# Other places for block 1's half points in the mixer blocks of a streaming attention and retention kernel

## The chip, the cores and the metric

The kernel is one program on one core of a Trainium2 chip. The metric is the device time of one execution in microseconds (us), and the median over the runs is what is compared. The engines are named as in the profile: PE (TensorE), DVE (VectorE), ACT (ScalarE), POOL (GpSimd, which here only issues gathers) and SP (which only issues other transfers).

## The reference, cut to what matters

One inference step of an encoder layer over nine blocks of 128 tokens: block 0 holds the sample rows, blocks 1 to 8 the prompt. All arrays are float32.

```python
h  = rmsnorm(x);  z = h @ w_in                       # q, k, v of A; q, k, v, gate of B; branch gates
oa = sliding_window_attention(z, sinks)              # mixer A, 8 heads, ALiBi, softmax
ob = groupnorm(retention(z)) * silu(z_rg)            # mixer B, 4 heads, state carried from block to block
x  = x + (sigmoid(ga) * (oa @ w_branch_a) + sigmoid(gb) * (ob @ w_branch_b)) @ w_out
h2 = rmsnorm(x)
idx, gate = top16_of_product_keys(h2 @ w_q)          # 8 heads x 16 experts = 128 rows a token
act = gelu(h2 . peer_u[idx])                         # "dots"
y  = x + sum_k gate_k * act_k * peer_v[idx_k]        # "values"
```

A mixer block takes the z of 128 tokens through attention, retention, the merge of the two branches and the output projection. The experts of a token block need 128 gathered rows of `peer_u` and 128 of `peer_v` for each token.

## The kernel before, in words

The kernel runs in stages. The one in question is the mixers of blocks 2 to 8. It is written as one Python loop per engine, so the order on each engine is fixed by hand, and semaphores tie the engines together. In the same stage runs what is left of block 1's expert work: 80 gathered rows of `peer_u` and 80 of `peer_v` for each token. It is cut into groups of three rows and spread over the mixer blocks as "half points".

`dve_point(v, blk, j)` (j from 0 to 7) is one half point. An odd j takes the dots of one group: three multiply-and-sum instructions (line 1472) over the buffers `ru`. An even j takes the values of a group that is four groups older: three multiply-and-add instructions (line 1489) over the buffers `rv`, and point 0 also one small product (line 1480). There are three buffers for each kind. So POOL may issue the three gathers of the next group only after the three instructions of this one are done. POOL's order is fixed, too: for each group number first the values' gathers (line 1508), then the dots' gathers (line 1516). Block 2 has only the dots; the last group of dots, in block 8, has two rows.

The order on DVE in `dve_block` for block b, with what the other engines do:

- copies of the transposed q and k (from line 689), which need PE's transposes (line 308) of this block; then block b-1's gating (line 429) and biases (line 433)
- point 0; then the scores are scaled and masked (lines 711 and 712, they need PE's line 623), `atm` is formed (line 714), row maxima (line 389 and on)
- ACT's exponentials (line 353) run, DVE takes point 1 and then waits for them (line 399); ACT scales the probabilities
- points 2 and 3; then `dve_merge` of block b-1 (lines 438 to 441), which needs PE's two branch products (lines 324 and 327). PE starts those when `atm` is written
- points 4 and 5; then the retention norm (lines 410 to 422), which needs PE's line 647
- points 6 and 7; then `dve_residual` of block b-1 (line 446), which needs PE's output product (line 340); the state update (line 735), which needs line 653; the second norm (lines 450 to 454)

PE's order in a block is: transposes (308), gated transposes of b-1 (315), scores (623, 346), branches of b-1 (324, 327), transposes of the probabilities (632), transposes of the merge (333), attention output (640), retention (646, 647), output product of b-1 (340), state product (653), then a wait for the retention norm.

SP's queue copies 40 parts of the expert table (`uv_d`, 1 MB each, lines 244 and 245), eight parts in each of the blocks 3 to 7, two at a time: after the load of the next keys part; after the probabilities (`prob`); after the merge's transposes (`mixt`), behind the next gates; and after the retention (`ro`).

```python
                        if blk > 2:
                            rest_of_table(sp, part, part + 2)
                            sp.wait_ge(s["prob"], blk + 1)
                            rest_of_table(sp, part + 2, part + 4)
```

After block 8 the stage closes with the last groups of values, block 1's output, the key search of block 2's tokens and the last merge; then the expert stage of blocks 2 to 8 begins.

## Time and profile before

| what | value |
|---|---|
| median of 3 runs | 4177.75 us (4168.81 to 4183.3) |
| the profiled execution | 4131.7 us, span 4129.9 us |
| granted TensorE clock, mean | 0.928 |
| busy share of the span | PE 80%, DVE 59%, POOL 43%, ACT 26% |
| bytes moved | 1563 MB, mean 378 GB/s |
| mixer stage of blocks 2 to 8 | from about 1165 to about 1676 us |

Times in the rows are us from the start of the span. A row of the timeline gives start, duration, engine, line, operation, output and inputs, and the count of instructions that it merges. In brackets stands how long the engine sat idle before it and on what. A releaser that begins with DMA is a transfer that landed late. Names of buffers carry the stage's suffix; `CUSTOM_DVE_ANT_0` is the dot instruction.

### The profile page before, as it was taken

To read this page: it belongs to the slowest core of one execution; us is meant where nothing else is said; L and a number is where in the kernel's file an instruction comes from. 1 tells how busy PE (TensorE), PEld (TensorE's weight loads), DVE (VectorE), ACT (ScalarE), POOL (GpSimd) and SP (SyncE) were. 2 spreads that over 40 slices of the span, in tenths; PEclk is the share of its full clock that TensorE was granted. 3 is DMA by queue.
4 is the path that set the end of the run, shared out by engine and by line. 5 is a ranking of instruction groups with operands and counts; after the bars stand their busy time and mean duration, and the time that the engine had idled before them with its cause. 6 is when DMAs were issued, how large, how long until landed. Compare 5 with 4: busy or idle time off the path is not lost.

```text
span 4129.9 us, 32128 instructions
## 1 busy us (share of the span) xinstructions
PE 3298.1 (80%) x8957; PEld 1643.4 (40%) x8957; DVE 2455.5 (59%) x4977; ACT 1088.2 (26%) x2932; POOL 1769.1 (43%) x1588
## 2 busy tenths in 40 slices
PE   8775589999928878749779779878878977977776
PEld 5453256666524444324224323323323423422222
DVE  0122168998857677544864764674684585485454
ACT  2102011111113233213333333333333333323322
POOL 1020137787723333114444454444444444445554
PEclk9876799999958888969999999999999999999999
DMA  9898899999999998469999999999999999999998
GB/s 352 297 290 310 321 304 413 411 407 414 412 360 341 344 354 300 160 269 420 421 421 418 415 420 399 421 414 409 420 409 409 419 417 403 422 406 422 422 422 353
DMA packets 303586, 1563.05 MB, mean 378 GB/s; under 512 B 31280, under 2 KB 59184, under 8 KB 179888
## 3 DMA queue, kind: packets, MB, share of 16 engines
q0 software_dynamic: 228096, 1300.34, 78.7%
q1 hardware_dynamic: 60736, 239.86, 15.0%
q10 hardware_dynamic: 14592, 21.10, 1.4%
q8 instruction: 51, 0.84, 0.1%
q14 instruction: 111, 0.91, 0.1%
HBM read 1517.54 MB, written 179.04 MB: 411 GB/s over the span
## 4 chain that ended last, share of the span: by engine, by line
DMA 26%; PE 18%; issue 7%; DVE 4%; ACT 1%; POOL 1%; POOLq 0%; ACTq 0%; DVEq 0%
DMA ring<-uv_d,IXD_p 26%; PE ps L1807 14%; PE ps L1779 3%; DVE ring L1906 2%; ACT dg L1850 1%; DVE BV_p L979 1%; POOL ring L2012 1%; ACT GE_p L1844 0%; DVE BP_p L984 0%; DVE CA_p L989 0%; DVE VV_p L1332 0%; DVE CA_p L1397 0%; DVE DOT_p L1906 0%; DVE ACC L1887 0%; PE ps L1796 0%
## 5 line engine op out<-in xcount | busy, mean ns | idle before, releaser
L1807 PE MATMUL ps<-ring,dg 128*128 128x512 f32 x3584 | 1704.6, 614 | 474.3 <-ACT dg L1850 449.9
L2012 POOL DMA_INDIRECT ring<-uv_d,IXD_p x896 | 1082.3, 1208 | 1318.1 <-PE ps L1807 1068.0
L1906 DVE CUSTOM_DVE_ANT_0 ring<-ring,H 128x1024 f32<-128x1024 f32 x896 | 1094.2, 1223 | 907.3 <-DMA ring<-uv_d,IXD_p 886.6
L1807 PEld LDWEIGHTS ps<-ring,dg 128*128 128x128 f32 x3584 | 664.0, 194 | 1432.8 <-ACT dg L1850 714.3
L1238 PE MATMUL ps<-w,xg 128*128 128x368 f32 x1792 | 554.3, 472 | 2.0 <-ACT SC_s L936 2.0
L1844 ACT ACTIVATE GE_p<-DOT_p 128x2 f32<-128x2 f32 x448 | 91.1, 203 | 1502.6 <-DVE DOT_p L1906 1502.6
L1238 PEld LDWEIGHTS ps<-w,xg 128*128 128x128 f32 x1792 | 340.4, 190 | 215.5 <-ACT SC_s L936 2.2
L1850 ACT ACTIVATE dg<-gdi,GE_p 128x128 f32<-128x128 f32 x896 | 310.6, 393 | 46.6 <-ACT GE_p L1844 1.2
L1838 ACT ACTIVATE gdi<-ident,GD_p 128x128 f32<-128x128 f32 x896 | 303.1, 386 | 26.3 <-issue 19.9
L145 POOL DMA_DIRECT2D uv_d<-in_peer_u x88 | 45.6, 518 | 504.7 <-DMA uv_d<-in_peer_v 270.3
L1779 PE MATMUL ps<-wq,hT_p 128*128 128x512 f32 x384 | 197.9, 597 | 0.0
L1508 POOL DMA_INDIRECT rv<-in_peer_v,IXD x80 | 88.4, 1105 | 231.6 <-DVE AC L1489 215.2
L969 POOL DMA_INDIRECT ring_s<-in_peer_v,IXD_s x128 | 158.2, 1236 | 44.9 <-issue 38.4
L1101 DVE CUSTOM_DVE_ANT_0 ring_s<-ring_s,H_s 128x1024 f32<-128x1024 f32 x128 | 152.1, 1223 | 41.6 <-DMA ring_s<-in_peer_u,IXD_s 40.5
L969 POOL DMA_INDIRECT ring_s<-in_peer_u,IXD_s x128 | 152.6, 1192 | 47.3 <-issue 40.2
L226 PE MATMUL ps<-w,xg 128*128 128x368 f32 x512 | 161.4, 479 | 13.9 <-DMA w<-in_w_in 13.9
L1112 DVE SCALAR_TENSOR_TENSOR ACC_s<-ring_s,WG_s,ACC_s 128x1024 f32<-128x1024 f32 x126 | 157.1, 1290 | 13.3 <-DMA ring_s<-in_peer_v,IXD_s 12.9
L1267 ACT ACTIVATE zo<-ps,rstd 128x368 f32<-128x368 f32 x112 | 61.8, 566 | 373.4 <-PE ps L1238 371.9
L1516 POOL DMA_INDIRECT ru<-in_peer_u,IXD x80 | 82.1, 1027 | 151.7 <-DVE DOT L1472 117.1
L1472 DVE CUSTOM_DVE_ANT_0 ru<-ru,H 128x1024 f32<-128x1024 f32 x80 | 96.0, 1222 | 60.0 <-DMA ru<-in_peer_u,IXD 59.9
L226 PEld LDWEIGHTS ps<-w,xg 128*128 128x128 f32 x512 | 98.6, 193 | 76.0 <-issue 16.3
L1489 DVE SCALAR_TENSOR_TENSOR AC<-rv,WG,AC 128x1024 f32<-128x1024 f32 x80 | 102.7, 1284 | 40.8 <-DMA rv<-in_peer_v,IXD 36.1
(415 smaller groups left out, 2901.7 us busy)
## 6 DMA issues: line engine op xcount, KB each, us to landing
uv_d<-in_peer_u POOLq DMA_DIRECT2D x88, 512.0 KB, 5.4
uv_d<-in_peer_v POOLq DMA_DIRECT2D x88, 512.0 KB, 6.6
w<-in_w_in SPq DMA_DIRECT2D x8, 2944.0 KB, 15.1
w<-in_w_in SPq DMA_DIRECT2D x16, 1472.0 KB, 9.8
z_d<-zo ACTq DMA_DIRECT2D x16, 1288.0 KB, 18.8
uv_d<-in_peer_u SPq DMA_DIRECT2D x40, 512.0 KB, 9.6
uv_d<-in_peer_v SPq DMA_DIRECT2D x40, 512.0 KB, 11.3
ring<-uv_d,IXD_p POOLq DMA_INDIRECT x896, 11.2
```

The lines of the kernel that those rows point to most:

```text
L226: mm = T.matmul(ps[:, m % AB, 0:WC], xg0[:, k, b * P:(b + 1) * P], w0[:, p % 2, n % 2, k, :], start=(k == 0), stop=(k == KT - 1))
L969: gather = g.indirect_dma_start(ring[:, n % RING, :], None, t["peer_u"] if kind == "u" else t["peer_v"], bass.IndirectOffsetOnAxis(ap=inde ...
L1101: V.tensor_tensor_reduce(out=row, in0=row, in1=H2[:], scale=1.0, scalar=0.0, op0=ALU.mult, op1=ALU.add, accum_out=DOT[:, k:k + 1]).then_in ...
L1112: V.scalar_tensor_tensor(ACC[:, k % 2], row, WG[:, k:k + 1], ACC[:, k % 2], ALU.mult, ALU.add).then_inc(d["freed"], 1)
L1238: mm = T.matmul(ps[:, n % AB, 0:WC], xg[:, k, b * P:(b + 1) * P], w[:, tile % 2, k, :], start=(k == 0), stop=(k == KT - 1))
L1489: V.scalar_tensor_tensor(AC1[:], row, WG1[:, k:k + 1], AC1[:], ALU.mult, ALU.add).then_inc(d["accz"], 1)
L1779: mm = T.matmul(bank(2 + n), hT[:, k, :], wq[:, k, n * 512:(n + 1) * 512], start=(k == 0), stop=(k == KT - 1))
L1807: mm = T.matmul(bank(6 + n), dg[:, k % DR, :], ring[:, k % RS, D + n * 512:D + (n + 1) * 512], start=(k == 0), stop=(k == NK - 1))
L1838: S.activation(gdi[:, k % GR, :], ident[:], ACT.Copy, scale=GD[:, k:k + 1]).then_inc(e["gdi"], 1)
L1850: S.activation(dg[:, k % DR, :], gdi[:, k % GR, :], ACT.Copy, scale=GE[:, k:k + 1]).then_inc(e["diag"], 1)
L1906: V.tensor_tensor_reduce(out=row, in0=row, in1=H2[:], scale=1.0, scalar=0.0, op0=ALU.mult, op1=ALU.add, accum_out=DOT[:, k:k + 1]).then_in ...
L2012: g.indirect_dma_start(ring[:, n % RS, :], None, uv_d, bass.IndirectOffsetOnAxis(ap=IXD[:, n:n + 1], axis=0)).then_inc(s_ring[n % RS], 16)
```

## The change

The half points keep their order among themselves and their content, and no instruction is added or removed. Their places in DVE's order are changed in each of the blocks 2 to 8. Point 1 goes ahead of the scores, point 2 into the wait for the exponentials, points 4 and 5 ahead of the merge, points 6 and 7 ahead of the retention norm.

```diff
-            dve_point(v, blk, 0)
+            for half_point in range(2):
+                dve_point(v, blk, half_point)
             if blk <= 2:
                 v.wait_ge(s_mask, 16 * 4 + 48 * blk)
             v.wait_ge(s["scores"], blk + 1)
...
             dve_softmax(v, blk, 2 * P, sink[:], step)
-            dve_point(v, blk, 1)
+            dve_point(v, blk, 2)
             dve_probs(v, blk, 2 * P, False)
-            for half_point in range(2, 4):
+            for half_point in range(3, 6):
                 dve_point(v, blk, half_point)
             if merge:
                 dve_merge(v, blk - 1)
-            for half_point in range(4, 6):
+            for half_point in range(6, 8):
                 dve_point(v, blk, half_point)
             v.wait_ge(s["oat"], blk + 1)
             V.tensor_copy(kaT[:, 0], kaT[:, 1])
             V.tensor_copy(va[:, 0], va[:, 1])
             dve_retention_norm(v, blk, 2, step)
-            for half_point in range(6, 8):
-                dve_point(v, blk, half_point)
             if merge:
                 dve_residual(v, blk - 1)
```

## Rows read from the trace of the kernel before

**Rows 1.** DVE's timeline in block 4, from its first copy to block 5's:

```profile
1309.77 0.68 DVE L689 COPY qbT_p<-ps 128x512 f32<-128x512 f32 x1
...
1316.79 4.06 DVE L1489 SCALAR_TENSOR_TENSOR AC<-rv,WG,AC 128x1024 f32<-128x1024 f32 x3
1321.20 1.22 DVE L711 SCALAR_TENSOR_TENSOR Pr_p<-ps,alibi_p 128x1024 f32<-128x1024 f32 x1 [0.35 <-PE ps L623]
...
1326.73 1.22 DVE L1472 CUSTOM_DVE_ANT_0 ru<-ru,H 128x1024 f32<-128x1024 f32 x1
...
1331.03 0.23 DVE L399 TENSOR_TENSOR rs_p<-rs_p,es_p 128x8 f32<-128x8 f32 x1 [0.78 <-ACT Pr_p L353]
...
1348.19 1.22 DVE L438 TENSOR_TENSOR gates_p<-gates_p,ps 128x1024 f32<-128x1024 f32 x1 [7.82 <-PE ps L327]
...
1379.56 1.23 DVE L1472 CUSTOM_DVE_ANT_0 ru<-ru,H 128x1024 f32<-128x1024 f32 x1 [0.80 <-DMA ru<-in_peer_u,IXD]
...
1380.71 1.22 DVE L446 TENSOR_TENSOR X_p<-X_p,ps 128x1024 f32<-128x1024 f32 x1
...
1384.98 0.68 DVE L689 COPY qbT_p<-ps 128x512 f32<-128x512 f32 x1
```

**Rows 2.** PE's timeline in block 4:

```profile
1324.21 10.14 PE L324 MATMUL ps<-wa_p,oaT_p 128*128 128x512 f32 x16 [1.04 <-DVE atm_p L714]
...
1351.85 1.09 PE L333 MATMUL ps<-ident,gates_p 128*128 128x128 f32 x8 [2.03 <-DVE gates_p L441]
1352.88 3.33 PE L640 MATMUL ps<-Pr_p,va 128*64 128x128 f32 x32
...
1373.42 1.89 PE L653 MATMUL ps<-zv_p,kdec_p 128*128 128x256 f32 x8
```

**Rows 3.** DVE's timeline, first copy and merge of block 3; end of block 7:

```profile
1236.81 0.68 DVE L689 COPY qbT_p<-ps 128x512 f32<-128x512 f32 x1
...
1273.62 1.22 DVE L438 TENSOR_TENSOR gates_p<-gates_p,ps 128x1024 f32<-128x1024 f32 x1 [4.70 <-PE ps L327]
...
1602.37 1.22 DVE L446 TENSOR_TENSOR X_p<-X_p,ps 128x1024 f32<-128x1024 f32 x1
...
1606.64 0.68 DVE L689 COPY qbT_p<-ps 128x512 f32<-128x512 f32 x1
```

**Rows 4.** PE's timeline, the state product of block 7:

```profile
1597.88 1.89 PE L653 MATMUL ps<-zv_p,kdec_p 128*128 128x256 f32 x8
```

**Rows 5.** Timeline of SP and POOL in block 4, first table copy, last gather:

```profile
1334.86 0.49 SPq L244 DMA_DIRECT2D uv_d<-in_peer_u  x1
...
1339.09 0.94 POOL L1508 DMA_INDIRECT rv<-in_peer_v,IXD  x1 [0.30 <-issue]
```

**Rows 6.** The tile rv, the gather issued at 1339.09 alone:

```profile
DMA to landing us min/median/max: 10.7/10.7/10.7
```

**Rows 7.** DVE's timeline at the end of block 8:

```profile
1670.55 1.22 DVE L446 TENSOR_TENSOR X_p<-X_p,ps 128x1024 f32<-128x1024 f32 x1 [5.33 <-PE ps L340]
```

**Rows 8.** Timeline of PE and POOL at the end of block 2:

```profile
1227.44 0.94 POOL L1508 DMA_INDIRECT rv<-in_peer_v,IXD  x1 [0.30 <-issue]
...
1231.82 3.01 PE L308 MATMUL ps<-ident,zqk_p 128*128 128x128 f32 x13 [18.59 <-DMA zqk_p<-z_d]
```

**Rows 9.** Block 2: busy of PE, PEld, DVE, ACT, POOL; PE clock, DMA share, GB/s:

```profile
1167.00:1232.00 65.00, 25.86 (x110) 22.32 (x111) 23.70 (x52) 15.12 (x34) 13.37 (x15) 0.58 1.00 400
```

**Rows 10.** DMA queues from 1165 to 1232: packets, MB, share:

```profile
q0 software_dynamic: 1713, 6.28, 23.4%
```

**Rows 11.** PE's timeline, in block 2 and behind block 8:

```profile
1201.85 6.00 PE L640 MATMUL ps<-Pr_p,va 128*64 128x128 f32 x32 [2.03 <-ACT Pr_p L676]
...
1715.28 3.68 PE L1546 MATMUL ps<-ident,zv_p 128*128 128x128 f32 x16 [5.33 <-ACT zv_p L1572]
```

**Rows 12.** PE in two stretches: length, PE busy, granted clock, DMA share, GB/s:

```profile
1575.20:1580.00 4.80, 4.80 (x34) 0.64 0.80 272
...
1715.30:1719.00 3.70, 3.70 (x17) 0.50 0.00 0
```

## The prediction

> **What bounds the kernel now.** The page of the profile says that the last stage, the experts of blocks 2 to 8, is nearly all transfers. The change does not touch that stage, so it moves the end only by moving its start. I therefore read the timeline of the mixer stage, engine by engine, and laid the landing of each gather beside it. Times below that begin with a plus are us behind the first copy (line 689) of a block.
>
> From block 3 to block 8 there are five turns, 369.8 us together [rows 3]. In block 4 the order of waits is this [rows 1, 2]. At +11.4 DVE has finished point 0 and waits 0.35 for the scores. At +17.0 it begins point 1, and still waits 0.78 for the exponentials. At +38.4, 7.8 late, it gets PE's branch products for the merge. At the end it waits for rows: the last dot of point 7 starts at +69.8, the moment its row has landed, and the residual follows at +70.9. The residual's own partner, PE's output product, ended where the state product begins, at +63.65. So the residual is 7.3 late for points 6 and 7. Over the five turns these lags are 6.6, 7.3, 6.8, 5.9 and 4.5, 31.1 in all (block 4's pair in [rows 1, 2], the last in [rows 3, 4]). Block 8 is different: there the residual waits 5.3 for PE, and PE bounds it [rows 7].
>
> **The change, part by part.** Nothing is added or removed: 80 dots of 1.22 and 80 values of some 1.3 us stay, and with them the gathers that POOL issues behind their semaphores. What changes is what stands ahead of what.
>
> *Points 6 and 7 ahead of the retention norm.* The norm's result is wanted by PE only after the state product, so there are some 10 us of cover. The residual can then start 0.2 behind PE's output product, as in block 8, instead of 31.1 late over five turns: 30.1 less. But the state update waits for the state product, which takes 1.9 [rows 2], where it now follows the residual at once, after 1.2. That gives 0.6 back in each block, as read from block 8's residual and update. Gain: 27.1 in five turns, 0 in block 8.
>
> *Point 1 ahead of the scores.* Three dots at a pitch of 1.15 are 3.4; DVE had 0.35 to spare there. So scores, `atm` and all behind them come 3.0 later: PE's branches start on `atm`, SP's second table copies start on the scaled probabilities. All of PE's chain to the output product hangs on that: 3.0 in each of six blocks, 15.0 in the five turns and 3.0 in block 8.
>
> *Point 2 in the exponentials' wait.* Three values take 4.0 until the next instruction may start. Point 1 and the wait had filled 4.3 there [rows 1]. Its gathers go out at +11.9 and have landed at +18.4 to +22.4 in all blocks, while point 2 wants them from +20.0 on, one each 1.3. No cost. If they were as late as the gathers that fly beside a table copy (10.7, [rows 6]), it would be 3.
>
> *Points 4 and 5 ahead of the merge.* The time to beat is PE's: +38.4 in block 4, +36.8 in block 3 [rows 1, 3], 37.6 on the mean of the five, plus the 3.0. DVE has time for the instructions; what counts is when rows land. Point 3 ends at +28.3, so POOL issues point 5's gathers at +29.1 to +31.6. SP's table copies now start at +28.15 (+25.1 before, and 3.0). In the kernel before, point 4's gathers have just this place: they follow 1.55 behind the first table copy of 1334.86, and the last goes out at 1339.09 and lands 10.7 later, 14.9 behind that copy [rows 5, 6]. In five blocks this distance is 14.3 to 14.9. What is in flight beside them is the same in both kernels: the end of one group, two parts of the table, this group. So point 5's last row lands at +42.75, the dot takes 1.22, and the merge starts at +44.0. That is 44.0 - 40.6 = 3.4 late on the mean: 17.1 in five turns. In block 8 point 5 has two rows, and other loads stand in place of the copies; the second row would land at +41.7 and the merge start at +42.9 instead of +41.4: 1.5. The bounds: 0 if the rows land as early as a gather does at the median (8.1 us), 3.4 + 1 if the half microsecond of queueing that I can't see adds up.
>
> *PE's clock.* PE waits for the merge 2.0 us now, at the full clock of 2.4 GHz [rows 2]. After the change it waits 4.6 to 6.3 in blocks 3 to 7 and 3.5 in block 8. After a wait of 5.33 the trace shows the granted clock at 0.50, that is 1.2 GHz, and 16 transposes took 3.68 [rows 11, 12]. Costs of such a fall: in block 7 it came at a wait of 2.0 already (granted 0.64 in that stretch) and cost some 1.6, block 6 likewise. If lines 333 and 640 run wholly at half clock, 640 takes 6.00 for 3.33 [rows 2, 11] and 333 about 0.9 more: 3.6. From below it is 0. I take 2.0, near to what was measured, in blocks 3 to 5, and 0.5 more in blocks 6 and 7, which have paid already: 7. At the start of a block PE's clock is low anyway, and is again.
>
> *Block 2.* It has dots only, and all of its transfers are squeezed: the share is 1.00 at 400 GB/s [rows 9]. Its points waited for rows one after another. Point 1 now fits whole into DVE's wait for block 2's scores, so each later group is asked for some ten us earlier. DVE doesn't gain by it. Block 3 starts when the keys part has landed, at 1231.8 [rows 8], and that load shares the engines with the gathers. Before, four groups had come through by then (6.28 MB, 1.57 each, [rows 10]) and the first values were only issued at 1227.4 [rows 8]. Now those values and the first dots of block 3 are also in flight ahead of it: up to 3.1 MB, 7.7 us at 400 GB/s. From below: if the keys part isn't delayed, block 3 starts 1.9 earlier, since DVE is no longer in the way. I take 5 later. The Trainium skill ("DMA: Bandwidth & Descriptors", on queues, rings and completion order) has each engine take turns between the queues that have work, a packet at a time. By that rule the gathers get half the engines while they last, the keys part is pushed back by nearly all of their bytes, and the term would be 6 to 7. By the lower bound of the rows it would be -1.9.
>
> **Sum.** -27.1 + 15.0 + 17.1 = +5.0 for the five turns; +4.5 for block 8; +7 for the clock; +5 for block 2: +21.5, all ahead of the expert stage, with nothing to absorb it. The profiled execution took 4131.7, 46 less than the median; I carry the difference over to the median: 4177.75 + 21.5 = 4199.
>
> **The rivals.** *A, the rows are in time (not slower).* If point 5's last row lands by +39.4, the merge doesn't wait for DVE, PE's clock stays, and what was gained at the block's end is kept: -27.1 + 15.0 + 2 + 3.0 - 1.9 = -9, 4169. For it speaks the median latency of 8.1. Against it is that in five blocks out of five the gathers behind this table copy took 14.3 to 14.9 behind its start. It decides at a merge start of about +42 on the mean: below, the five turns gain.
>
> *B, the clock holds.* The merge is late, but PE keeps 2.4 GHz over the wait: 7 less, +14.5, or +7.6 if block 2 gives nothing either: 4185 to 4192. For it speaks that block 4 passed its wait of 2.0 at full clock [rows 2]; against it the wait of 5.33 [rows 11].
>
> *C, the clock falls at every merge and stays low.* 3.6 in each block and, if it lasts to the retention or the output product, the 3.2 that line 324 pays for its slow start (10.14 for 16, against 6.9 at the pitch of the fast ones [rows 2]): up to 6.8 in place of 2, so 30 to 45 in all, 4208 to 4223. The Trainium skill ("TensorE: Matmul & The Clock Gate", on oscillation) says that a wait between two bursts, repeated in each turn of a loop, makes PE go cold in every one of them. By that rule all six blocks pay; the trace agrees for the wait of 5.33 and shows two of six already at 2.0.
>
> **Chances.** The forecast 0.46, with its own range +12 to +30; A 0.17; B 0.23; C 0.14. 0.3% is 12.5 us, about what runs of this kernel can tell. Slower by more than that: the forecast but for 0.03 of it, C, and 0.10 of B: 0.67. Within: 0.29. Faster: 0.04, the part of A that ends beyond its -9. The range goes from 4176, most of A left out, to 4222, C's end.
>
> **What would show it.** In the changed kernel, per block from 3 on: no idle time ahead of line 446 but for PE's line 340, and the residual right behind that product; line 711 three us later, with no wait for line 623; no wait for ACT at line 399; a wait for a `ru` row just ahead of the merge, the merge at +43 to +45, and no wait for line 327; PE's wait ahead of line 333 at 4.6 to 6.3; block 3's first copy near 1242; turns of 74 to 78 where they were 73 to 75. The forecast is wrong if the merge starts before +42, if PE's line 333 and 640 stay at 1.09 and 3.33 everywhere, or if block 3 begins by 1236.

## The result, and the profile after

| kernel | median of 8 runs | range |
|---|---|---|
| before | 4172.27 us | 4166.05 to 4183.59 |
| after | 4207.49 us | 4197.64 to 4232.85 |

The changed kernel takes 1.0092 times as long (95% interval 1.0064 to 1.012): 35 us slower by the two medians. Predicted were +21.5 and 4199 us, with a range up to 4222. Two executions in the chip's slower state, 4603 us of p67_only and 4193 us of late7_head, are in no ratio and no median below. In the changed kernel the lines behind 711 are one or more off (711 is 712, 1472 is 1471, 1489 is 1488, 1508 is 1507); lines 308 to 699 are the same.

DVE's timeline in block 4 of the changed kernel, to compare with [rows 1]:

```profile
1379.53 0.68 DVE L689 COPY qbT_p<-ps 128x512 f32<-128x512 f32 x1
...
1393.97 1.22 DVE L712 SCALAR_TENSOR_TENSOR Pr_p<-ps,alibi_p 128x1024 f32<-128x1024 f32 x1
...
1403.79 0.17 DVE L399 TENSOR_TENSOR rs_p<-rs_p,es_p 128x8 f32<-128x8 f32 x1 [0.23 <-ACT Pr_p L353]
...
1409.78 1.28 DVE L1488 SCALAR_TENSOR_TENSOR AC<-rv,WG,AC 128x1024 f32<-128x1024 f32 x1 [2.03 <-DMA rv<-in_peer_v,IXD]
1415.29 1.29 DVE L1488 SCALAR_TENSOR_TENSOR AC<-rv,WG,AC 128x1024 f32<-128x1024 f32 x1 [4.22 <-DMA rv<-in_peer_v,IXD]
1418.33 1.28 DVE L1488 SCALAR_TENSOR_TENSOR AC<-rv,WG,AC 128x1024 f32<-128x1024 f32 x1 [1.75 <-DMA rv<-in_peer_v,IXD]
1420.84 1.23 DVE L1471 CUSTOM_DVE_ANT_0 ru<-ru,H 128x1024 f32<-128x1024 f32 x1 [1.23 <-DMA ru<-in_peer_u,IXD]
...
1423.43 1.23 DVE L1471 CUSTOM_DVE_ANT_0 ru<-ru,H 128x1024 f32<-128x1024 f32 x1 [1.36 <-DMA ru<-in_peer_u,IXD]
...
1425.81 1.22 DVE L438 TENSOR_TENSOR gates_p<-gates_p,ps 128x1024 f32<-128x1024 f32 x1
...
1453.66 1.22 DVE L446 TENSOR_TENSOR X_p<-X_p,ps 128x1024 f32<-128x1024 f32 x1 [9.30 <-PE ps L340]
...
1458.53 0.68 DVE L689 COPY qbT_p<-ps 128x512 f32<-128x512 f32 x1
```

The end of the turn is what was forecast: the residual (line 446) waits for PE's product alone, and no row is late there. The price stands ahead of the merge. The scores come at +14.4 instead of +11.4, without a wait; then five rows in a row are late, and the merge starts at +46.3, where PE's branches end at +40.0. DVE stood idle for 10.6 us in front of it, all for rows. The last row of point 5 is not one of them: it was there when DVE came to it, at +45.1.

PE's timeline in the same block, to compare with [rows 2]:

```profile
1396.97 8.86 PE L324 MATMUL ps<-wa_p,oaT_p 128*128 128x512 f32 x16 [4.04 <-DVE atm_p L715]
...
1429.47 1.97 PE L333 MATMUL ps<-ident,gates_p 128*128 128x128 f32 x8 [8.16 <-DVE gates_p L441]
1431.37 4.87 PE L640 MATMUL ps<-Pr_p,va 128*64 128x128 f32 x32
...
1453.46 1.89 PE L653 MATMUL ps<-zv_p,kdec_p 128*128 128x256 f32 x8
```

And two stretches of it: length, busy time of PE, PEld, DVE, ACT and POOL, then the granted clock, DMA share and GB/s:

```profile
1421.50:1429.40 7.90, 0.00 (x0) 0.00 (x0) 6.51 (x10) 1.79 (x2) 4.24 (x5) 0.68 0.79 245
1429.50:1436.10 6.60, 6.60 (x40) 6.16 (x40) 6.39 (x8) 1.02 (x1) 2.33 (x3) 0.61 0.97 308
```

PE does nothing for 7.9 us, and the granted clock falls meanwhile. Line 333 then takes 1.97 where it took 1.09, line 640 4.87 for 3.33. Read in finer stretches, the granted clock is 1.00 from 1421.6 to 1423, 0.50 from 1425 to 1434 and 1.00 again from 1436.2.

The timeline of SP and POOL in block 4, to compare with [rows 5]:

```profile
1407.56 0.49 SPq L244 DMA_DIRECT2D uv_d<-in_peer_u  x1
...
1404.37 1.89 POOL L1507 DMA_INDIRECT rv<-in_peer_v,IXD  x1 [4.55 <-DVE AC L1488]
1406.57 1.99 POOL L1507 DMA_INDIRECT rv<-in_peer_v,IXD  x1 [0.30 <-issue]
1408.86 0.94 POOL L1507 DMA_INDIRECT rv<-in_peer_v,IXD  x1 [0.30 <-issue]
1410.11 1.77 POOL L1515 DMA_INDIRECT ru<-in_peer_u,IXD  x1 [0.30 <-issue]
1412.18 0.94 POOL L1515 DMA_INDIRECT ru<-in_peer_u,IXD  x1 [0.30 <-issue]
1413.43 0.94 POOL L1515 DMA_INDIRECT ru<-in_peer_u,IXD  x1 [0.30 <-issue]
```

The copies go out at +28.0, as predicted. POOL issues point 4's values and point 5's rows, six gathers, as one train around them. Three of the six take 1.8 to 2.0 us to issue instead of 0.94, so the last goes out at +33.9.

The load of the next keys part in block 2, in the kernel before and in the changed one, and the start of block 3 in the changed one, to compare with [rows 8]:

```profile
1212.55 2.30 SPq L751 DMA_DIRECT2D zqk_p<-z_d  x1
...
1275.28 1.19 SPq L750 DMA_DIRECT2D zqk_p<-z_d  x1
...
1298.63 3.00 PE L308 MATMUL ps<-ident,zqk_p 128*128 128x128 f32 x13 [24.44 <-DMA zqk_p<-z_d]
...
1301.67 0.69 DVE L689 COPY qbT_p<-ps 128x512 f32<-128x512 f32 x1 [3.96 <-PE ps L308]
```

Block 2 started at 1234.81 here. The keys part lets PE begin 63.8 behind that, where it was 56.7 before. Of these 7.1, 3.0 are that SP asks for the part later, at +40.5 instead of +37.5, and 4.1 that PE gets it 23.4 behind that instead of 19.3. DVE's first copy then follows sooner, so block 2's turn is 66.86 for 61.72.

**Where the time is.** The sum, from the first copy of block 2 to the last residual of the mixers, in us (first copies as in [rows 3, 8], each kernel by its own trace):

| stretch | before | after | difference | predicted |
|---|---|---|---|---|
| block 2's turn | 61.72 | 66.86 | +5.1 | +5 |
| turns of blocks 3 to 7 | 369.83 | 392.15 | +22.3 | +12 |
| block 8 to the last residual | 177.56 | 184.80 | +7.2 | +4.5 |
| sum | | | +34.7 | +21.5 |

That is close to the 35 of the medians, in part by luck: the last row also holds the stretch from block 8's own residual on, which differs by 4 us or more between traces (see p1_only), and the stretch behind the last residual, which the table leaves out, is 5.4 longer (2351.1 for 2345.7). The profiled executions themselves differ by 100 us (spans 4129.9 and 4229.7). Some 60 of these lie ahead of block 2, in code that the change does not touch: the costliest groups of the two pages have the same matmuls with another idle time ahead of them. Before:

```profile
L1238 PE MATMUL ps<-w,xg 128*128 128x368 f32 x1792 | 554.3, 472 | 2.0 <-ACT SC_s L936 2.0
```

After:

```profile
L1237 PE MATMUL ps<-w,xg 128*128 128x368 f32 x1792 | 581.9, 483 | 63.7 <-issue 61.3
```

This is no effect of the change, as the runs below show, and I read everything else relative to a block's first copy.

### The profile page after: what moved, and what is told of

It reads as the page before. It is cut to its first block, busy times and chain, and to the rows that moved or that the text cites. A ratio compares the mean times of both kernels' runs of the same rounds, so it can differ in the third digit from the quotient of the medians.

```text
span 4229.7 us, 32134 instructions
## 1 busy us (share of the span) xinstructions
PE 3329.0 (79%) x8957; PEld 1656.0 (39%) x8957; DVE 2452.3 (58%) x4977; ACT 1089.9 (26%) x2932; POOL 1759.3 (42%) x1588
## 3 DMA queue, kind: packets, MB, share of 16 engines
q1 hardware_dynamic: 60736, 239.86, 14.9%
## 4 chain that ended last, share of the span: by engine, by line
DMA 25%; PE 17%; issue 7%; DVE 5%; ACT 1%; POOL 1%; POOLq 0%; ACTq 0%; DVEq 0%
DMA ring<-uv_d,IXD_p 25%; PE ps L1806 14%; PE ps L1778 3%; DVE ring L1905 2%; ACT dg L1849 1%; DVE BV_p L978 1%; POOL ring L2011 1%; DVE BP_p L983 0%; DVE CA_p L988 0%; ACT GE_p L1843 0%; DVE CA_p L1396 0%; DVE DOT_p L1905 0%; DVE VV_p L1331 0%; DVE ACC L1886 0%; PE ps L1795 0%
## 5 line engine op out<-in xcount | busy, mean ns | idle before, releaser
L2011 POOL DMA_INDIRECT ring<-uv_d,IXD_p x896 | 1070.8, 1195 | 1334.6 <-PE ps L1806 1086.7
L1237 PE MATMUL ps<-w,xg 128*128 128x368 f32 x1792 | 581.9, 483 | 63.7 <-issue 61.3
L1507 POOL DMA_INDIRECT rv<-in_peer_v,IXD x80 | 103.5, 1294 | 311.3 <-DVE AC L1488 294.8
L968 POOL DMA_INDIRECT ring_s<-in_peer_u,IXD_s x128 | 150.3, 1175 | 71.4 <-issue 39.2
L968 POOL DMA_INDIRECT ring_s<-in_peer_v,IXD_s x128 | 148.4, 1160 | 61.8 <-issue 38.1
L226 PE MATMUL ps<-w,xg 128*128 128x368 f32 x512 | 160.6, 477 | 13.9 <-DMA w<-in_w_in 13.9
L1100 DVE CUSTOM_DVE_ANT_0 ring_s<-ring_s,H_s 128x1024 f32<-128x1024 f32 x128 | 150.7, 1220 | 17.8 <-DMA ring_s<-in_peer_u,IXD_s 11.1
L1471 DVE CUSTOM_DVE_ANT_0 ru<-ru,H 128x1024 f32<-128x1024 f32 x80 | 95.1, 1224 | 42.1 <-DMA ru<-in_peer_u,IXD 34.2
```

Source lines behind the costliest of these rows:

```text
L226: mm = T.matmul(ps[:, m % AB, 0:WC], xg0[:, k, b * P:(b + 1) * P], w0[:, p % 2, n % 2, k, :], start=(k == 0), stop=(k == KT - 1))
L968: gather = g.indirect_dma_start(ring[:, n % RING, :], None, t["peer_u"] if kind == "u" else t["peer_v"], bass.IndirectOffsetOnAxis(ap=inde ...
L1100: V.tensor_tensor_reduce(out=row, in0=row, in1=H2[:], scale=1.0, scalar=0.0, op0=ALU.mult, op1=ALU.add, accum_out=DOT[:, k:k + 1]).then_in ...
L1237: mm = T.matmul(ps[:, n % AB, 0:WC], xg[:, k, b * P:(b + 1) * P], w[:, tile % 2, k, :], start=(k == 0), stop=(k == KT - 1))
L1507: g.indirect_dma_start(rv[:, k % PG, :], None, t["peer_v"], bass.IndirectOffsetOnAxis(ap=IXD1[:, AHEAD + k:AHEAD + k + 1], axis=0)).then_i ...
L2011: g.indirect_dma_start(ring[:, n % RS, :], None, uv_d, bass.IndirectOffsetOnAxis(ap=IXD[:, n:n + 1], axis=0)).then_inc(s_ring[n % RS], 16)
```

## The experiments

All were timed in five rounds beside the kernel before. Diffs are against the kernel that is named. The ratios are to the kernel before on the same chip. The last three columns are from one trace each. "Block 8" runs from its first copy to the last residual of the mixers.

| run | ratio, 95% interval | median less before | block 2 | blocks 3 to 7 | block 8 |
|---|---|---|---|---|---|
| before (its trace) | | | 61.72 | 369.83 | 177.56 |
| after (its trace) | 1.0092, 1.0064 to 1.012 | +35.2 | 66.86 | 392.15 | 184.80 |
| p1_only | 1.0058, 1.0045 to 1.0071 | +23.9 | 67.09 | 384.14 | 176.55 |
| p45_only | 1.0069, 1.0056 to 1.0082 | +29.1 | 61.75 | 387.71 | 182.25 |
| p67_only | 1.007, 1.0057 to 1.0083 | +29.0 | 67.75 | 391.06 | 176.81 |
| copies_late | 1.005, 1.0037 to 1.0063 | +21.7 | 66.54 | 368.98 | 182.49 |
| warm | 1.0067, 1.0053 to 1.008 | +29.1 | 66.66 | 377.25 | 184.99 |
| p1_back | 1.0106, 1.0088 to 1.0125 | +42.2 | 68.49 | 387.41 | 182.46 |
| b3_on | 1.0082, 1.0066 to 1.0097 | +36.0 | 61.70 | 388.35 | 183.75 |
| late7 | 0.9983, 0.9973 to 0.9992 | -6.5 | 61.18 | 361.17 | 176.90 |
| after_again | 1.012, 1.0082 to 1.0157 | +50.1 | 67.10 | 389.63 | 186.78 |
| all_three | 1.0056, 1.0028 to 1.0085 | +22.1 | 61.01 | 369.53 | 184.42 |
| late7_head | 0.9966, 0.9937 to 0.9995 | -10.0 | 63.16 | 356.48 | 175.11 |
| late7_fill76 | 0.9955, 0.9941 to 0.9968 | -20.5 | 61.64 | 349.31 | 171.74 |

### One part at a time

**p1_only**, against the kernel before: points 0 and 1 ahead of the scores, none in the exponentials' wait.

```diff
-            dve_point(v, blk, 0)
+            for half_point in range(0, 2):
+                dve_point(v, blk, half_point)
...
-            dve_point(v, blk, 1)
```

> Point 1 alone is moved, ahead of the scores. My theory: scores, atm, branches and all of PE's chain come 3.0 us later in each of the blocks 3 to 8, and the gathers of points 4 to 7 with them, so nothing gives it back: 6 x 3.0 = 18. Block 2 adds up to 5 as in the changed kernel, since its gathers go out earlier and push back the load of the next keys part. Together +18 to +23 against the kernel before; line 711 at +14.4 behind a block's first copy, line 438 at about +41. Rival 1, the loss of the change lies outside the mixer blocks: within 5 of 0. Rival 2, the rows of points 6 and 7 set a turn's end whatever stands ahead of them: under +8.

Block 2 pays 5.4 and the five turns 14.3 by the traces: the scores are at +14.4, and the merge at +41.2 in block 4 with DVE waiting 9.0 for PE. The 15.0 of the sum, and the +5 of block 2, are right, and point 1's move in block 2 is enough for the whole of the latter. The last column shows -1.0 where 3.0 was expected. Block 8's own residual is 3.5 later (+67.4 for +63.9), but the stretch behind it is 4.5 shorter (109.2 for 113.7): PE's transposes in line 1546 follow without a wait and take 2.01, where in the kernel before they wait 5.33 and take 3.68 [rows 11]. In the fourteen traces that stretch is between 109.2 and 115.3, so the last column can't be read finer than that.

**p45_only**, against the kernel before: points 4 and 5 ahead of the merge.

```diff
-            for half_point in range(2, 4):
+            for half_point in range(2, 6):
                 dve_point(v, blk, half_point)
             if merge:
                 dve_merge(v, blk - 1)
-            for half_point in range(4, 6):
-                dve_point(v, blk, half_point)
```

> Points 4 and 5 alone are moved, ahead of the merge. My theory: point 5's rows land at +42 to +44.5, where they do in the kernel before, so the merge starts at about +45.7 instead of 37.6 on the mean, 8 late; PE waits 8 to 10 us ahead of line 333, its clock falls to half, and lines 333 to 647 cost 2 more. The rows of points 6 and 7 are then there early and the residual follows PE's output product, which gives 5 back. Turn 78 to 79 instead of 74: +24 for five turns, +7 for block 8, together +31. Rival 1 (the loss of the change is all point 1's, and the merge has slack): within 8 of 0. Rival 2 (loss outside the mixer blocks): within 5 of 0.

The merge is at +44.0 to +46.1 though SP's copies start 3 earlier than in the changed kernel; PE waits 8.2 to 10.3, and line 333 takes 1.97 in every block. The turns of blocks 3 to 7 grow by 17.9 together. And the residual, at +71.6 to +73.7, starts 0.2 behind PE's output product in every block, although points 6 and 7 stand where they stood.

**p67_only**, against the kernel before: points 6 and 7 ahead of the norm.

```diff
-            for half_point in range(4, 6):
+            for half_point in range(4, 8):
                 dve_point(v, blk, half_point)
...
             dve_retention_norm(v, blk, 2, step)
-            for half_point in range(6, 8):
-                dve_point(v, blk, half_point)
```

> Points 6 and 7 alone are moved, ahead of the retention norm, with 4 and 5 still behind the merge. My theory: their rows can't be there before +57 to +70, since POOL asks for them only when point 4 is done; the norm waits for them until +71, PE waits for the norm ahead of the next transposes, and the turn grows by about 5: +25, with +4 from block 2. Rival (moving 6 and 7 off the block's end is the gain of the change by itself, 27 in five turns): -20 or better.

Block 2 pays 6.0 here, with point 1 in its old place. PE's timeline of p67_only at the start of block 3 has what it waits for, not the keys part but the retention norm, which stands behind the rows of point 7:

```profile
1240.85 3.04 PE L308 MATMUL ps<-ident,zqk_p 128*128 128x128 f32 x13 [28.09 <-DVE yn_p L422]
```

DVE's timeline of p67_only at the end of block 4, which began at 1320.77:

```profile
1376.46 1.28 DVE L1489 SCALAR_TENSOR_TENSOR AC<-rv,WG,AC 128x1024 f32<-128x1024 f32 x1 [6.84 <-DMA rv<-in_peer_v,IXD]
...
1389.41 1.23 DVE L1472 CUSTOM_DVE_ANT_0 ru<-ru,H 128x1024 f32<-128x1024 f32 x1 [0.81 <-DMA ru<-in_peer_u,IXD]
...
1390.83 1.42 DVE L410 BATCH_NORM_STATS2 stats_p<-ps 128x6 f32<-128x256 f32 x4
...
1395.20 1.21 DVE L446 TENSOR_TENSOR X_p<-X_p,ps 128x1024 f32<-128x1024 f32 x1
```

Point 7's last row lands at +68.6, little sooner than before (+69.8). Only now the norm stands behind it, 4.4 us until the residual, which starts at +74.4 instead of +70.9. So it is not the place of points 6 and 7 that gave the changed kernel its punctual residual; it is that points 4 and 5 have run earlier and taken the requests of 6 and 7 along, as p45_only shows. The five turns of the three parts alone sum to +14.3 + 17.9 + 21.2 = +53.4, and together they are +22.3, 31 less. p1_back below has all but point 1's move, and its five turns are +17.6, where those of p45_only and p67_only sum to +39.1. So 21.5 of the 31 lie between points 4 and 5 and points 6 and 7 (with point 2, which p1_back moves as well), and the rest is point 1's.

### What delays the merge

**copies_late**, against the changed kernel: SP's two table parts behind the probabilities go to those behind the mixed rows' transposes.

```diff
                             sp.wait_ge(s["prob"], blk + 1)
-                            rest_of_table(sp, part + 2, part + 4)
...
-                            rest_of_table(sp, part + 4, part + 6)
+                            rest_of_table(sp, part + 2, part + 6)
```

> The changed kernel, and SP's two table parts that follow the scaled probabilities are issued with the two that follow the merge's transposes. My theory (point 5's rows queue behind those copies): point 5's last row lands by +37, the merge starts when PE's branches are ready, about +39.8 instead of 45.4; PE waits 2.0 ahead of line 333 and keeps 2.4 GHz, so lines 333 to 647 take 7.8 us instead of 9.9: 7.7 less in each of five turns, 38 less than the changed kernel, within 8 of the kernel before. Rival 1 (the merge is late by POOL's order and the latency of a gather itself): as the changed kernel, +35. Rival 2 (the bytes of a turn bound it, and they only come later): half of it, +15 to +20.

The merge comes at +39.2, 41.8, 42.1, 41.3 and 42.9 in blocks 3 to 7, on the mean 3.9 earlier, and the five turns fall from 392.15 to 368.98, the level of the kernel before. DVE's timeline in block 4 of copies_late, which began at 1313.47:

```profile
1336.36 1.28 DVE L1488 SCALAR_TENSOR_TENSOR AC<-rv,WG,AC 128x1024 f32<-128x1024 f32 x1 [1.38 <-DMA rv<-in_peer_v,IXD]
...
1354.07 1.23 DVE L1471 CUSTOM_DVE_ANT_0 ru<-ru,H 128x1024 f32<-128x1024 f32 x1 [0.29 <-DMA ru<-in_peer_u,IXD]
...
1355.22 1.22 DVE L438 TENSOR_TENSOR gates_p<-gates_p,ps 128x1024 f32<-128x1024 f32 x1
...
1370.57 1.23 DVE L1471 CUSTOM_DVE_ANT_0 ru<-ru,H 128x1024 f32<-128x1024 f32 x1 [5.47 <-DMA ru<-in_peer_u,IXD]
```

Point 5's last row is now 0.29 late, but point 2's rows wait (1.38) and point 7's do (5.47). So the copies do hold the rows up, and moving them is worth 23 us of turns: 19.8 for the merge, 3.4 for PE from line 333 to line 340, which follows shorter waits (2.1 to 4.0). But the bytes that were moved make other rows late. My bound for this run, within 8 of the kernel before, was too bold: block 2 (+4.8) and block 8 (+4.9) keep their losses, since there are no such copies in them, and the stretch behind the last residual is 9.9 longer, which I have not traced further.

**p1_back**, against the changed kernel: point 1 behind the scores again.

```diff
-            for half_point in range(2):
+            for half_point in range(0, 1):
                 dve_point(v, blk, half_point)
...
-            dve_point(v, blk, 2)
+            for half_point in range(1, 3):
+                dve_point(v, blk, half_point)
```

> The changed kernel with point 1 put back behind the scores: one half point ahead of the scores, two in the exponentials' wait, three ahead of the merge, two behind it. Scores at +11.4 and PE's branches 3.0 earlier; point 2 and the exponentials' sums as late as in the changed kernel or 0.7 later, so SP's table copies and point 5's gathers where they were. Theory (point 5's rows set the merge, PE's branches have some 5.6 us to spare): merge at +44.5 to +46, turns 78 to 79, within 5 us of the changed kernel. Rival (the 3.0 of the scores is a term of its own in each block, as my prediction's sum had it): 15 to 18 below the changed kernel.

The scores are back at +11.4, PE's branches start 3.0 earlier, and little comes of it: the merge is at +43.1 to +45.9, PE waits 8.8 to 9.9 ahead of line 333, the five turns take 387.4 for 392.15 and 389.63. The merge is set by rows. The 3.0 of point 1 and the lateness of the merge are one delay that I had split in two, as the prediction's merge start of +44.0 says; removing one part lets the other grow. Block 2 is 6.8 above the kernel before: PE waits there for the retention norm behind points 6 and 7, as in p67_only.

**b3_on**, against the changed kernel: block 2 in the old order.

```diff
-            for half_point in range(2):
+            for half_point in range(1 if blk == 2 else 2):
                 dve_point(v, blk, half_point)
...
-            dve_point(v, blk, 2)
+            dve_point(v, blk, 1 if blk == 2 else 2)
             dve_probs(v, blk, 2 * P, False)
-            for half_point in range(3, 6):
+            for half_point in range(*((2, 4) if blk == 2 else (3, 6))):
                 dve_point(v, blk, half_point)
...
-            for half_point in range(6, 8):
+            for half_point in range(*((4, 6) if blk == 2 else (6, 8))):
                 dve_point(v, blk, half_point)
...
             dve_retention_norm(v, blk, 2, step)
+            if blk == 2:
+                for half_point in range(6, 8):
+                    dve_point(v, blk, half_point)
```

> The changed kernel with block 2 in the old order, blocks 3 to 8 in the new one. Theory (block 3 starts later because the gathers asked for earlier in block 2 push back the keys part): block 2's turn back from 66.9 to some 62, the later turns as in the changed kernel, 4 to 6 us below it. Rival (what block 2 gains is given back, since the load that ends it is late for all the bytes that block 2 must move by then, or block 3 then waits for its rows): 0 to 2 below it.

Block 2's turn is 61.70, as in the kernel before, and the five turns stay at 388.35. The timing, 1.0082, can't tell 5 us from the changed kernel on another chip; the trace has the 5.2.

### What the clock costs

**warm**, against the changed kernel: the probabilities' transposes are done four times over, into the same places, before PE signals them.

```diff
-            for n in range(2 * HA):
+            for n in range(2 * HA * (4 if blk > 2 else 1)):
+                n %= 2 * HA
```

> The changed kernel, but PE transposes the scaled probabilities four times over in blocks 3 to 8 (the same 16 into the same banks, 64 in all) before it signals them, so that it works through most of its wait ahead of line 333. Output as before. Theory (the clock falls in that wait, and costs what lines 333 and 640 take longer): the wait shrinks from 7.3 to some 2 us, line 333 goes from 1.97 to 1.1, line 640 from 5.2 to 3.3-3.7, the span from line 333 to line 340 from 10.6 back to some 8.3 as in the kernel before, and the residual, which waits 9 us for PE alone, starts 2 to 2.5 earlier in each of six blocks: 12 to 15 us below the changed kernel, some 20 above the kernel before. Rival (the end of the block is bound by transfers, PE's speed there is given back as a wait for rows or for the next block's columns): lines 333 and 640 get faster, the turns stay at 78 to 79, less than 4 us below the changed kernel. A loss would show as ACT's copies of the transposed probabilities coming late ahead of line 640.

PE's timeline of warm in block 5, which began at 1393.22; lines behind 632 are one on:

```profile
1433.77 7.15 PE L633 MATMUL ps<-ident,Pr_p 128*128 128x128 f32 x64
1441.86 1.09 PE L333 MATMUL ps<-ident,gates_p 128*128 128x128 f32 x8 [0.93 <-DVE gates_p L441]
1442.95 3.33 PE L641 MATMUL ps<-Pr_p,va 128*64 128x128 f32 x32
```

The merge is nearly as late as in the changed kernel (+44.3 to +45.4), only PE has been at work until shortly ahead of it, and line 333 is 1.09 in all six blocks, line 640 (here 641) at 3.33 again. From line 333 to line 340 PE takes 8.0 on the mean of five blocks for 10.6, and the turns fall by 14.9 against the changed kernel's first trace, 12.4 against its second. More work on PE made the turns shorter; by the medians warm is 7 and 13 us below b3_on and p1_back, which ran on the same chip, though neither is the changed kernel itself. Of the 14.9, 12.9 are PE's stretch and 2.0 a merge that is 0.4 earlier. That settles the clock's term as real. Its size moves between executions: against the 8.49 of the kernel before, the 10.6 of the first trace is 2.1 in a turn, 10.5 in five, and the 10.0 of the second (after_again) is 1.5 in a turn.

**after_again**: the changed kernel, unaltered, on the chip of the two runs that follow in the table.

> The changed kernel once more, unaltered, beside the kernel before on this chip, since its variants were timed on other chips than it was. Theory (its loss is the mixers' alone and is the same on every chip): 33 to 40 us above the kernel before; five turns of 388 to 392 us. Rival (part of the 35 was of its own chip): 25 to 30 above, like its parts done alone.

The ratio, 1.012, agrees with the first within their intervals, though the 50 us of the medians are more than the 33 to 40 that I expected, and the mixers agree with the first trace: 67.1, 389.6, 186.8. Its trace has the idle time ahead of block 2 again, and so have the traces of all_three and late7_head on that chip, with 53.2 and 58.4 us, kernels with other orders. In all other traces it is 2.0, also in those of warm, copies_late, p1_back and b3_on, which have most of the changed order. The kernel before has a median of 4128 to 4129 beside those runs, 4165 beside these three and 4172 in the first comparison. So it does not go with the order of the half points. Nor does it go with the chip alone: late7_fill76 ran on the chip with the same number some twelve minutes later, and there the kernel before took 4128 and the trace has 2.0.

**all_three**, against the changed kernel: the edits of copies_late and b3_on, and the transposes twice over (three times in block 8).

> The changed kernel with its three costs taken back that earlier runs separated: SP's two table parts behind the probabilities moved to those behind the mixed rows' transposes, PE's probability transposes done twice over (three times in block 8) so that it works through its wait ahead of line 333, and block 2 in the old order. Theory (the costs are separate and add up): from the changed kernel's +35 to +38 come off 23 for the copies in five turns, 5 for block 2, and 2.5 in each of six blocks for the clock, 15 in all: within 8 of the kernel before, five turns 356 to 362, block 8's residual at +70. Rival (with the copies moved, rows of other points are what a turn waits for, so the clock's part is given back there): five turns stay at 366 to 369, +12 to +17 in all. A second rival: the time goes to the expert stage, since SP's table parts end later; the stretch behind the last residual would be 8 or more longer than the 2345.7 of the kernel before.

The rival held. Line 333 takes 1.09 in four blocks of six, and the five turns still take 369.5, as copies_late alone; the kernel is 22 us above the one before, where the rival had 12 to 17. In blocks 4 and 7 the merge is back at +45. DVE's timeline in block 4, which began at 1354.64:

```profile
1378.58 1.28 DVE L1492 SCALAR_TENSOR_TENSOR AC<-rv,WG,AC 128x1024 f32<-128x1024 f32 x1 [1.58 <-DMA rv<-in_peer_v,IXD]
...
1398.46 1.22 DVE L1475 CUSTOM_DVE_ANT_0 ru<-ru,H 128x1024 f32<-128x1024 f32 x1 [0.79 <-DMA ru<-in_peer_u,IXD]
1399.62 1.21 DVE L438 TENSOR_TENSOR gates_p<-gates_p,ps 128x1024 f32<-128x1024 f32 x1
```

Of the twelve rows of points 2 to 5 in this block, eleven are waited for. Once the copies are moved, the rows of points 2 to 5 set the pace: in the five turns PE's stretch from line 333 to line 340 is 6.2 shorter than in copies_late, and the merges are 6.7 later. The three costs are separate in their causes but don't add up.

### A kernel that beats both

**late7**, against the kernel before: point 7 goes behind the residual, the state update and the second norm.

```diff
             dve_retention_norm(v, blk, 2, step)
-            for half_point in range(6, 8):
+            for half_point in range(6, 7):
                 dve_point(v, blk, half_point)
...
             if merge:
                 dve_norm2(v, blk - 1)
+            for half_point in range(7, 8):
+                dve_point(v, blk, half_point)
```

> The kernel before with one thing changed: point 7 goes behind the residual, the state update and the second norm of the block, point 6 stays where it was. Theory (in blocks 3 to 7 of the kernel before the residual is 4.5 to 7.3 late for point 7's rows, and nothing else binds the block's end): the residual starts 0.2 to 2 behind PE's output product, turns 70 to 72 instead of 73 to 75, 10 to 20 us below the kernel before. Rival (the turn is bound by its transfers, some 25 MB at about 400 GB/s plus waits of the queues, so that rows come late at the next point): turns of 73 to 75, within 4 us of the kernel before. A second rival: the next block's copies and scores now wait behind point 7's last rows, and it costs up to 3 a turn, 5 to 15 above the kernel before.

In blocks 3 to 7 the residual starts at +63.5 to +64.7 and waits 0.3 to 2.7 for PE's product, as expected, but the turns only fall from 74.0 to 72.2, and the kernel gains 6.5 us, where 10 to 20 were expected. Point 7's dots now stand ahead of the next block's first copy. They hold it back: PE's transposes for block 5 end at 1371.7, and DVE comes to them at 1376.88. PE waits through that, 9.3 us. PE's timeline of late7 at the start of block 5:

```profile
1370.10 1.58 PE L308 MATMUL ps<-ident,zqk_p 128*128 128x128 f32 x13
1380.96 1.97 PE L315 MATMUL ps<-ident,gates_p 128*128 128x128 f32 x8 [9.28 <-DVE gates_p L429]
1382.86 5.65 PE L623 MATMUL ps<-kaT,qaT_p 64*128 64x256 f32 x16
```

The granted clock of the last stretch of that wait and of what follows:

```profile
1377.50:1379.50 2.00, 0.00 (x0) 0.00 (x0) 0.86 (x3) 1.99 (x3) 1.43 (x2) 0.50 1.03 422
1379.50:1385.00 5.50, 4.04 (x14) 3.34 (x16) 5.29 (x9) 3.07 (x5) 1.91 (x2) 0.50 1.01 406
```

Since warm had shown that such a wait can be filled, I filled this one.

**late7_head**, against late7: PE transposes the identity into a free bank during the waits ahead of lines 315 and 324.

```diff
             pe_transposes(pe, blk, half)
+            if merge and blk > 2:
+                pe.wait_ge(s["x1"], blk - 1)
+                for n in range(60):
+                    T.transpose(ps[:, 7, 0:P], ident[:], ident[:])
...
             pe_scores_b(pe, blk)
+            if merge and blk > 2:
+                for n in range(40):
+                    T.transpose(ps[:, 7, 0:P], ident[:], ident[:])
```

> The kernel before with point 7 behind the second norm, and in blocks 3 to 8 PE fills two of its waits with transposes of the identity into a bank that is free there: 60 ahead of the gated rows' transposes (line 315), 40 ahead of its wait for the decayed scores (line 324). Output as before. Theory (the granted clock of 0.50 from line 315 to the start of line 324 is what these waits cost): line 315 at 1.1 for 1.97, line 623 at some 2.8 for 5.65, line 324 at 6.9 for 9.1 to 10.2, branches 2 to 3 earlier, merge 2 to 3 earlier since DVE waits 5 to 8 for them; of this a residual that already waits 0.3 to 2 for rows keeps half: turns of 70 to 71.5 for 72, 4 to 12 us below the same kernel without the fill, 10 to 18 below the kernel before. Rival (rows and DVE set the turn now, PE's branches only move the merge): the merge comes 2 to 3 earlier, turns stay at 72, within 3 of the kernel without the fill.

Five turns of 356.5 for 361.2. Where the clock held (blocks 5 and 7) line 324 started at +14.2 and took 7.1, and the merge was at +35.2. In all of blocks 4 to 8 a wait of 2.73 was left ahead of line 315. In blocks 4, 6 and 8 the granted clock fell to 0.50 in it or right behind it, lines 623 and 346 took 5.0 to 5.7 and 2.1, and with the second fill behind them line 324 started at +16.6 to +18.2.

**late7_fill76**, against late7_head: the first fill is 76.

```diff
-                for n in range(60):
+                for n in range(76):
```

> The kernel with point 7 behind the second norm and PE's two fills, with 76 transposes instead of 60 in the first. Theory (with 60 a wait of 2.7 us is left ahead of line 315, and in four of six blocks the granted clock falls in it, so that line 324 starts at +16.6 to +18.2 instead of +14.2; with 76 some 0.9 is left and the clock holds): line 315 at 1.1 and line 324 at +14.2 to +14.7 and 7.0 long in all blocks from 4 on, merge at +35 to +36 in all, turns of 70 to 71 (five turns 351 to 355, where 60 gave 356.5 and no fill 361.2), 12 to 22 us below the kernel before. Rival (rows set the turn): merge at +35, five turns stay at 355 to 357, 6 to 14 below.

PE's timeline of late7_fill76 in block 6:

```profile
1450.79 1.09 PE L315 MATMUL ps<-ident,gates_p 128*128 128x128 f32 x8 [0.98 <-DVE gates_p L429]
1451.81 2.96 PE L627 MATMUL ps<-kaT,qaT_p 64*128 64x256 f32 x16
1454.70 1.16 PE L346 MATMUL ps<-qbT_p,kbT_p 128*128 128x128 f32 x8
1455.70 4.53 PE L633 MATMUL ps<-ident 128*128 128x128 f32 x40
1460.94 5.42 PE L324 MATMUL ps<-wa_p,oaT_p 128*128 128x512 f32 x12 [0.72 <-DVE atm_p L722]
```

The clock holds in blocks 4 to 8: the merge is at +35.2 in all of them, the turns 69 to 70.6, and the five together 349.3, a little below what was expected. The kernel is 0.45% below the kernel before (ratio 0.9955, 0.9941 to 0.9968), 20.5 us by the medians. The changed kernel is 35 above the same kernel, so some 55 lie between the two, though they were not timed side by side. The residual waits 0.6 to 4.1 for PE; rows are not what it starts on.

## Why the prediction was right, point by point

**The direction and the waits were right, the gain was put down to the wrong points, and two terms of the sum were too small.** The change costs 35 us, which is above the +12 to +30 that the forecast named as its own and in what rival C had. That the time of 4207 lies in the forecast's range up to 4222 is in part luck: the kernel before came out 5 us faster than in the runs that the prediction started from. For the five turns:

| term | predicted | measured |
|---|---|---|
| residual right behind line 340 | -27.1 | -27.1 |
| scores 3.0 later | +15.0 | +15.0 |
| merge late behind the start of line 324 | +17.1 | +23.9 |
| PE's clock, line 333 to line 340 | +7 | +10.5 |
| sum | +12.0 | +22.3 |

*The residual.* It starts 0.2 behind PE's product in every block. The amount was right, but the step "Points 6 and 7 ahead of the retention norm [...] Gain: 27.1" was not. p45_only has the same punctual residual with points 6 and 7 in their old place, and p67_only shows that their new place alone costs 21 in the five turns. The gain is that of points 4 and 5, whose earlier end lets the last rows be asked for earlier. The number came out right because both were moved.

*Scores.* As worked out: no wait at line 712, line 324 at +17.4. p1_only has the same 3.0 a block alone. p1_back shows that in the changed kernel it is no longer a cost of its own, since the rows set the merge.

*The merge.* The term that was furthest off rests on the step "POOL issues point 5's gathers at +29.1 to +31.6". They go out at +30.6 to +33.9 in block 4, and the last at +33.6 to +33.9 in four of the five, at +32.6 in block 3. The time from issue to landing was right as far as this trace has it, some 11 (assumed 11.1): block 4's second row of point 5 was asked for at +32.7, and DVE's wait for it ended at +43.9, 11.25 later. I had taken 0.94 for each issue; in all five blocks the first two of point 4's values take 1.9 and 2.0 and point 5's first row 1.45 to 1.8. Point 4's gathers and point 5's now go out back to back, so every long issue ahead delays those behind it. The prediction also had the last row set the merge. In none of the five blocks does DVE wait for that row: the last wait is for the second row of point 5 in blocks 3, 4 and 6 and for the first in blocks 5 and 7, and from there two or three dots at 1.2 each are left. The merge was at +45.4 on the mean instead of +44.0: 1.4 in five turns is the 6.8 that was missing. That these rows are late because of SP's copies is shown by copies_late, which brings them 3.9 forward.

*The clock.* A fall at every merge, in all six blocks, after waits of 6.7 to 8.2 (predicted 4.6 to 6.3, as the merge was later). Blocks 3 to 5 paid 2.4 to 2.9, where I had 2.0, blocks 6 and 7 1.0 to 1.3, where I had 0.5. Rival C had the fall right and its length wrong: line 340 takes 13.90 in every block, so the clock is back by then. The Trainium skill ("TensorE: Matmul & The Clock Gate", on oscillation) says that every round of such a loop starts cold; by the rows above it does. By warm the term is shown, not only read.

*Block 8.* Its own residual is 7.6 later: 3.0 for the scores, 3.2 for the merge (1.5 predicted), 1.4 for the clock (the prediction has a wait of 3.5 there and no term for it, without a reason). Of this 7.2 reaches the last residual.

*Block 2.* +5.1 for +5, with block 3's first copy where it was expected. p1_only has it with point 1 alone moved, b3_on takes it away. The prediction has it all as the gathers' bytes ahead of the keys part. By the two rows of that load, 3.0 of the 7.1 that PE starts later are a later issue, which the prediction did not have, and 4.1 a longer flight. That the flight is longer because the gathers compete with it remains an inference: no run changed the bytes ahead of that load without changing the order. And p67_only and p1_back show a second limit, which the prediction did not have either: with points 6 and 7 ahead of the norm, PE waits for the norm at the start of block 3, and block 2 is 6.0 and 6.8 longer. In the changed kernel the keys part comes last and hides it.

*The rivals.* A needed the merge at +40.6, and it came 4.8 later. B is out: line 333 takes 1.97 in every block. The 35 us lie within C's 30 to 45, because its two parts, a late merge and a fall in every block, were both there, the merge 1.4 later than predicted and the clock at some 2 us a block, where C had 3.6 to 6.8.

## What to carry to other kernels

When work is moved ahead of a wait, ask not only whether there is time for it, but when its data can have landed: its requests move with it, and here they came to stand behind other copies and in one long train on the queue that issues them. Parts of a reordering don't add: each alone cost 24 to 29 us, together 35. Run a part alone before you give it the gain: here the gain came from other points than the ones it was put down to. A long wait of PE can cost twice, once as a wait and once in the matmuls behind it, here 1.0 to 2.9 us behind waits of 6.7 to 8.2. If it can't be removed, filling it with harmless transposes is worth trying, and the length has to be tried out: with 60 transposes a wait of 2.73 was left and the clock fell in three blocks of five, with 76 a wait of 0.98 and it held in all five.

## What the runs showed of the hardware that was not expected

- The granted clock is not a function of the wait's length alone. Behind the same wait of 2.73 us in late7_head it fell to 0.50 in three blocks and held in two; in block 3 of warm it held at 1.00 over a wait of 3.07. After 2.03 ahead of line 333 in the kernel before, line 640 took 3.33 in four blocks of six and 4.75 and 4.97 in blocks 6 and 7. After the waits of 6.7 us and more in the changed kernel it had fallen every time.
- A gather that takes 0.94 us to issue on POOL takes 1.8 to 2.0 at some places of the order, often the same place in each turn: the second of the three that go out behind point 6, for one, took 1.99 in all five turns of the changed kernel. What it waits for, the trace doesn't say, and no run tested it.
- In the stage ahead of the mixers PE can stand idle for some 2.03 us ahead of single matmuls, one after another, with nothing that the profile shows to wait for: 63.7 and 67.4 us in all in the two traces of the changed kernel, 53.2 and 58.4 in two others taken beside the second, 2.0 in the other ten, one of them on a chip with the same number. PE's timeline of the changed kernel in that stage:

```profile
653.66 0.77 PE L1237 MATMUL ps<-w,xg 128*128 128x368 f32 x1 [2.03 <-issue]
656.46 0.77 PE L1237 MATMUL ps<-w,xg 128*128 128x368 f32 x1 [2.03 <-issue]
```

It is larger than everything else that this study measures. Whoever compares two profiles should first see whether their difference lies in the code that was changed. Its cause stays open.
